# A mixture-of-experts layer that adds its gated expert rows up in DRAM by accumulating scatters

## What is computed

```python
top_logit, top_e = lax.top_k(logits, TOP_K)
gates = jax.nn.softmax(top_logit, axis=-1)
...
xs = xf[tok]
hu = lax.ragged_dot(xs, w_gate_up, group_sizes) + b_gate_up[e_sorted]
gate = jnp.minimum(hu[:, :D_FF], SWIGLU_LIMIT)
up = jnp.clip(hu[:, D_FF:], -SWIGLU_LIMIT, SWIGLU_LIMIT)
act = (up + 1.0) * gate * jax.nn.sigmoid(SWIGLU_ALPHA * gate)
y = lax.ragged_dot(act, w_down, group_sizes) + b_down[e_sorted]
y = y * g_sorted[:, None].astype(y.dtype)
out = jnp.zeros_like(xf).at[tok].add(y)
...
h = layer_norm(ALPHA_RES * h + ffn, ln2_g[l], ln2_b[l])
```

## Time and profile before

| what | value |
|---|---|
| median of 3 runs | 4528.06 us (4527.1 to 4535.33) |
| profiled execution: span | 4529.3 us |
| busy share of the span: PE, DVE, ACT, POOL | 95%, 68%, 40%, 22% |
| mean granted TensorE clock | 0.972 |
| projection; attention; routing; experts; last stage, ends in the profile | about 643; 1840; 1854; 4387; 4529 us |
| DMA over the span | 665.72 MB, 147 GB/s |

### The profile page before, as it was taken

How to read it: one execution, slowest core, us unless ns; L and a number is a source line. 1 busy time by engine, 2 the same in 40 slices (tenths; PEclk the granted TensorE clock), 3 DMA queues, 4 the chain that set the end, 5 groups by cost and what they waited for, 6 DMA issues and landing times. The chain is left out here.

```text
span 4529.3 us, 70549 instructions
## 1 busy us (share of the span) xinstructions
PE 4289.9 (95%) x24356; PEld 3153.5 (70%) x24356; DVE 3076.1 (68%) x4861; ACT 1817.6 (40%) x2677; POOL 1010.1 (22%) x1152
## 2 busy tenths in 40 slices
PE   8999988999999998699999999999999999999987
PEld 4444434444444454599989889899999999999961
DVE  2587867878888873555556556666676777777768
ACT  1222223443434433233434444444445555555530
POOL 1111101221111122211112212222222222222235
PEclk9999989999999999799999999999999999999986
DMA  6443330120110010544555456474657667667668
GB/s 194 126 122 92 87 101 16 30 27 21 18 23 16 14 27 19 148 158 148 174 168 190 155 183 220 162 250 161 237 197 239 208 230 241 219 234 237 212 214 362
DMA packets 534140, 665.72 MB, mean 147 GB/s; under 512 B 64416, under 2 KB 402592, under 8 KB 533952
## 3 DMA queue, kind: packets, MB, share of 16 engines
q1 hardware_dynamic: 419664, 501.02, 34.7%
q10 hardware_dynamic: 87744, 77.15, 5.4%
q0 software_dynamic: 26576, 85.56, 5.0%
HBM read 543.61 MB, written 120.03 MB: 147 GB/s over the span
## 5 line engine op out<-in xcount | busy, mean ns | idle before, releaser
L2000 PE MATMUL gu<-x_hi,w_hi 128*128 128x240 f32 (+8 forms) x4096 | 1196.5, 292 | 4.1 <-issue 4.1
L2003 PE MATMUL gu<-x_lo,w_hi 128*128 128x240 f32 (+8 forms) x4096 | 1195.5, 292 | 0.5 <-issue 0.5
L2004 PE MATMUL gu<-x_hi,w_lo 128*128 128x240 f32 (+8 forms) x4096 | 1194.1, 292 | 0.0
L2106 DVE TENSOR_TENSOR w_lo<-w_raw,w_hi 128x2048 fp32r<-128x2048 f32 x386 | 874.6, 2287 | 414.1 <-ACT w_hi L2190 386.2
L2190 ACT ACTIVATE w_hi<-w_raw 128x2048 fp32r<-128x2048 f32 x386 | 726.8, 1908 | 207.4 <-PE gu L2004 132.0
L2000 PEld LDWEIGHTS gu<-x_hi,w_hi 128*128 128x128 f32 x4096 | 774.7, 189 | 4.5 <-issue 4.3
L2003 PEld LDWEIGHTS gu<-x_lo,w_hi 128*128 128x128 f32 x4096 | 773.3, 189 | 1.1 <-issue 0.9
L2004 PEld LDWEIGHTS gu<-x_hi,w_lo 128*128 128x128 f32 x4096 | 773.8, 189 | 0.0
L1972 POOL TENSOR_TENSOR a_lo<-up,a_hi 128x384 fp32r<-128x384 f32 x256 | 396.6, 1549 | 1177.8 <-ACT a_hi L2202 1177.8
L570 PE MATMUL proj_acc<-w_in_sb,hT 128*128 128x512 f32 (+1 forms) x1280 | 499.0, 537 | 0.7 <-ACT hT L586 0.7
L2000 PE MATMUL yp<-w_hi,a_hi 128*128 128x512 f32 x1088 | 445.6, 410 | 2.3
(11 more groups left out here) (316 smaller groups left out, 5878.6 us busy)
## 6 DMA issues: line engine op xcount, KB each, us to landing
w_raw<-w_gate_up SPq DMA_DIRECT2D x258, 1024.0 KB, 7.6
w_raw<-w_down SPq DMA_DIRECT2D x128, 1024.0 KB, 8.1
y_dram<-y_rows ACTq DMA_DIRECT2D x128, 256.0 KB, 2.6
y_dram<-zeros ACTq DMA_DIRECT2D x12, 2688.0 KB, 15.5
h_blk<-h_dram SPq DMA_DIRECT2D x32, 512.0 KB, 8.7
qi_dram<-qi_stage ACTq DMA_DIRECT2D x16, 640.0 KB, 3.2
x_in<-x SPq DMA_DIRECT2D x16, 512.0 KB, 6.1
w_in_sb<-w_in SPq DMA_DIRECT2D x4, 2048.0 KB, 14.2
```

The costliest lines, as they stand in the source:

```text
L2000: op = nc.tensor.matmul(out, s_hi_, m_hi, start=(n == 0), stop=False)
L2003: nc.tensor.matmul(out, s_hi_, m_lo, start=False, stop=False)
L2004: op = nc.tensor.matmul(out, s_lo_, m_hi, start=False, stop=(n == len(pairs) - 1))
L2106: nc.vector.tensor_tensor(w_lo[:, c % 2, cols], raw[:, c % 3, cols], w_hi[:, c % 2, cols].bitcast(F32), ALU.subtract).then_inc(s_lo, 1)
```

## The change

Every token gets a row in a new DRAM tensor, `sums`, in which `h1` is written first, beside its place of old. A list entry now holds the token and its gate, divided by `ALPHA_RES`. ACT multiplies a strip by the gates when it copies it out of PSUM, and POOL, in place of ACT and SP, adds the strip to its tokens' rows of `sums` by indirect scatters that accumulate. The unused places of a list name rows behind the last token, with gate 0. `hold` fetches a visit's tokens and gates out of the list buffer before the next gather overwrites it, and waits until the last visit's scatters have landed; it and the gather now stand before j = 3 of POOL's loop. For the third tile of rows, SP loads the list in four pieces and a small table of constants (`load_third`). The last stage loads `sums` where it gathered, PE makes the bias alone, and the finish on DVE has two operations where it had three. The first norm's factor `ALPHA_RES` is divided out of the variance's epsilon. What served the old way (the positions, their round trip through DRAM, the zeros in `y_dram`) goes.

The diff, cut to its core:

```diff
 project_stage, on ACT
-                        nc.scalar.dma_start(D_["y"][row:row + SHARE, :].rearrange("(p n) (c d) -> p (n c) d", n=SHARE_N, d=P),
-                                            zeros[0:shape[0]].unsqueeze(1).broadcast_to(shape)).then_inc(s_clear, 16)
 attend_stage, on SP
-                sp.dma_start(D_["lists"][0:EXPERTS * SEQ, :].rearrange("(p n) o -> p (n o)", p=P),
-                             res[:, 0:EXPERTS * SEQ // P].bitcast(I32)).then_inc(s_clear, 16)
...
+                sp.dma_start(D_["lists"].rearrange("(p a n) o -> p a (n o)", p=CLEARED, a=2),
+                             res[0:CLEARED, 0:2 * ROWS].bitcast(I32).unsqueeze(1).broadcast_to(shape)
+                             ).then_inc(s_clear, 16)
+                for name in ("h1", "sums"):
+                    sp.dma_start(D_[name][SEQ:, :].rearrange("(m p) n -> p m n", p=P),
+                                 res[:].unsqueeze(1).broadcast_to([P, 1 + ROWS // P, D])).then_inc(s_clear, 16)
...
-                    sp.dma_start(D_["h1"][b * P:(b + 1) * P, :], h1[:]).then_inc(s_h1st, 16)
+                    for name in ("h1", "sums"):
+                        sp.dma_start(D_[name][b * P:(b + 1) * P, :], h1[:]).then_inc(s_h1st, 16)
 attend_stage, on DVE (weigh)
+                    nc.vector.tensor_copy(entry[:, :, 0], token[:, b:b + 1].broadcast_to([P, TOP_E]))
...
+                    nc.vector.tensor_scalar(entry[:, :, 1].bitcast(F32), e_gate, e_inv, 1.0 / ALPHA_RES,
+                                            ALU.mult, ALU.mult).then_inc(s_at, 1)
 experts_stage, on SP (store_third and the round trip of the positions go)
+                def load_third(v):
+                    at = look_up(sp, v, 1, MOST)
                     rest, few = (look_up(sp, v, what, 1) for what in (2, 3))
+                    if not first(v):
+                        sp.wait_ge(s_hold, v)
                     for i in range(4):
+                        row = at + 2 * P + i * FEW - rest * ((i - i % 2) * FEW) - few * (i % 2 * FEW)
+                        sp.dma_start(third[i * FEW:(i + 1) * FEW], D_["lists"][bass.ds(row, FEW), :]
+                                     ).then_inc(s_third, 16)
+                    sp.dma_start(spot[:], A["spots"][bass.ds(rest + few, 1)].rearrange("o p j n -> (o p) j n")
+                                 ).then_inc(s_third, 16)
 
                 def body(v):
...
                         if first(v) and c == 0:
                             sp.wait_ge(s_who, 16)
+                            load_third(0)
                         if first(v) and c == 1:
                             sp.wait_ge(s_x, 48)
-                        if not first(v) and c in (3, 4):
-                            store_third(v - 1, 2 if c == 3 else 5)
+                        if c == 5:
+                            load_third(v + 1)
                         chunk(v, c, e)
 experts_stage, on POOL
+                def hold(v):
+                    if not first(v):
+                        pool.wait_ge(s_yst[0], 32 * v)
+                        pool.wait_ge(s_yst[1], 32 * v)
+                        pool.wait_ge(s_yst[2], 48 * v)
+                    pool.wait_ge(s_third, 80 * v + 80)
+                    nc.gpsimd.tensor_tensor(scaled[:], spot[:, :, 0], third[:, 0:1].broadcast_to([P, 3]), ALU.mult)
+                    for h in range(2):
+                        nc.gpsimd.tensor_scalar(at_main[:, :, h], who[:, 0:2, 0], 2.0, float(h), ALU.mult, ALU.add)
+                    nc.gpsimd.tensor_copy(gate_now[:, 0:2], who[:, 0:2, 1].bitcast(F32))
+                    nc.gpsimd.tensor_copy(gate_now[:, 2:3], third[:, 1:2].bitcast(F32))
+                    pool.drain()
+                    nc.gpsimd.tensor_tensor(at_third[:], scaled[:], spot[:, :, 1], ALU.add).then_inc(s_hold, 1)
+                    pool.drain()
+                def scatter(v, n):
+                    pool.wait_ge(s_y, 6 * v + n + 3)
+                    nc.gpsimd.tensor_tensor(idle[:, n:n + 1], zero[:, 0:1], zero[:, 0:1], ALU.add)
+                    if n % 3 < 2:
+                        parts = [(halves, at_main[:, n % 3, n // 3:n // 3 + 1], y[:, n % 3])]
+                    elif n == 2:
+                        parts = [(quarters, at_third[:, w:w + 1], y[:, 2, w * BANK // 2:(w + 1) * BANK // 2])
+                                 for w in range(2)]
+                    else:
+                        parts = [(halves, at_third[:, 2:3], y[:, 2])]
+                    for rows, at, part in parts:
+                        nc.gpsimd.indirect_dma_start(rows, bass.IndirectOffsetOnAxis(ap=at, axis=0), part, None,
+                                                     compute_op=ALU.add).then_inc(s_yst[n % 3], 16)
                 def body(v):
-                    gather(v + 1)
+                    if not first(v):
+                        scatter(v - 1, 5)
                     for j in range(J):
+                        if j == 3:
+                            hold(v)
+                            gather(v + 1)
                         pool.wait_ge(s_ah, 8 * v + j + 1)
                         nc.gpsimd.tensor_tensor(a_lo[:, j], up[:, j % 2], a_hi[:, j].bitcast(F32), ALU.subtract)
                         nc.gpsimd.tensor_copy(a_rest[:, j], up[:, j % 2, 2 * P:2 * P + REST]).then_inc(s_al, 1)
+                    for n in range(5):
+                        scatter(v, n)
 experts_stage, on ACT (store)
-                        act.wait_ge(s_yst[slot], (32, 32, 192)[slot] * v + (0, 0, 0, 16, 16, 128)[n])
-                    nc.scalar.activation(y[:, slot], yp[:, n % 2], ACT.Copy).then_inc(s_y, 1)
-                    if n % 3 < 2:
-                        act.wait_ge(s_y, 6 * v + n + 3)
-                        nc.scalar.dma_start(
-                            D_["y"][bass.ds(v * ROWS + (n % 3) * P, P), (n // 3) * BANK:(n // 3 + 1) * BANK], y[:, slot]
-                        ).then_inc(s_yst[slot], 16)
+                        act.wait_ge(s_yst[slot], (32, 32, 48)[slot] * v + (0, 0, 0, 16, 16, 32)[n])
+                    if n == 0:
+                        act.wait_ge(s_hold, v + 1)
+                    nc.scalar.activation(y[:, slot], yp[:, n % 2], ACT.Copy, scale=gate_now[:, slot:slot + 1]
+                                         ).then_inc(s_y, 1)
 combine_stage, on SP (AHEAD is 6)
                     if t >= AHEAD:
-                        sp.wait_ge(s_tot, t - AHEAD + 1)
-                    sp.dma_start(h1[:, t % AHEAD], D_["h1"][t * P:(t + 1) * P, :]).then_inc(s_h1[t % AHEAD], 16)
+                        sp.wait_ge(s_st[slot], 16 * (t // AHEAD))
+                    sp.dma_start(total[:, slot], D_["sums"][t * P:(t + 1) * P, :]).then_inc(s_in[slot], 16)
 combine_stage, on POOL
-                    for k in range(TOP_E):
-                        nc.gpsimd.indirect_dma_start(
-                            rows[:, t % AHEAD, k], None, D_["y"],
...
 combine_stage, on DVE
-                    nc.vector.scalar_tensor_tensor(total[:, slot], h1[:, at], ALPHA_RES, acc[:, t % SUMS],
-                                                   ALU.mult, ALU.add).then_inc(s_tot, 1)
+                    nc.vector.tensor_tensor(row, row, acc[:, slot], ALU.add).then_inc(s_tot, 1)
...
+                    nc.vector.scalar_tensor_tensor(row, row, small[:, slot, 12:13], gain[:], ALU.subtract, ALU.mult)
+                    dve.drain()
                     dve.wait_ge(s_rstd, t + 1)
-                    nc.vector.tensor_scalar(total[:, slot], total[:, slot], small[:, slot, 12:13], small[:, slot, 15:16],
-                                            ALU.subtract, ALU.mult)
-                    dve.drain()
-                    nc.vector.tensor_tensor(total[:, slot], total[:, slot], gain[:], ALU.mult)
-                    dve.drain()
-                    nc.vector.tensor_tensor(total[:, slot], total[:, slot], bias[:], ALU.add).then_inc(s_out, 1)
+                    nc.vector.scalar_tensor_tensor(row, row, small[:, slot, 15:16], bias[:], ALU.mult, ALU.add
+                                                   ).then_inc(s_out, 1)
```

More of the change, by code:

```diff
@@ L90, in project_stage @@
     GAPS = 16
-    CLEARS = 12
-    SHARE = (MAX_VISITS - EXPERTS) * ROWS // CLEARS
-    SHARE_N = next(n for n in range(1, SHARE + 1) if SHARE % n == 0 and SHARE // n <= P)
-    assert SHARE * CLEARS == (MAX_VISITS - EXPERTS) * ROWS
     CHUNKS = [(n * BANK, min(BANK, IN_W - n * BANK)) for n in range(5)]
@@ L1609, in half @@
                             act.wait_ge(s_clear, CLEARS)
-                        wait(act, s_h1st, 16 * k)
+                        wait(act, s_h1st, 32 * k)
                         wait(act, s_ht, 2 * k)
@@ L1765, in _ @@
                 nc.vector.tensor_scalar(here[:], until[:], visit_no[:], None, ALU.is_gt)
-                nc.vector.scalar_tensor_tensor(table[:, 1], expert_no[:], float(SEQ), table[:, 1], ALU.mult, ALU.add)
+                nc.vector.scalar_tensor_tensor(table[:, 1], expert_no[:], float(LISTED), table[:, 1], ALU.mult, ALU.add)
```

(17 more changed lines are left out.)

219 lines of the change are left out of this document (63 added, 156 removed).

## The result

The changed kernel takes **4538.2 us** (median of 20 runs, 4530.8 to 4548.6) against 4528.6 us for the kernel before (20 runs beside them): a ratio of **1.0019**, 95% interval 1.0012 to 1.0026. The forecast was 4512 us, faster. It is slower by a fifth of a per cent. This small change of the time hides two large ones of opposite sign. The profiled execution spans 4536.6 us, 7.3 more than that of before.

What follows compares the result with a forecast made beforehand. PE was taken to bound the experts, with POOL's `a_rest` last in its chain, and DMA the last stage. -35.8 + 4.5 + 11 + 2 + 2 = -16.3 us from 4528.06 gave 4512 us, range 4492 to 4550.

Steps and rivals of the forecast that it cites:

- Last stage: Stage after the experts: gathers go, DVE sets the pace at 5.62 us a tile; 142.2 to 106.4 us, gain 35.8.
- Seam: Between experts and last stage: POOL's last accumulating scatter must land; 8.6 us against 4.1, +4.5 us.
- Visits: Experts stage: POOL's block before j = 3 makes 12 width-240 visits 0.9 us late each; +11 us, bounds 0 and 64.
- `hold`, six small operations and two drains, about 1.4 us: POOL before j = 3: estimated from `who_now`, 0.19 us apiece, plus gaps; part of a 12.1 us block against 10.38 of room.
- 0.81 us of DVE's slack: DVE's idle time before the gate of j = 7 in a width-240 visit, taken off the 1.7 us overrun, leaving 0.9.
- Start and attention: Before the first gate: +2 us at the experts' start (0 to 4) and +2 in attention (0 to 6).
- the first (the block fits): Rival, POOL before j = 3: chain 0.9 us shorter, no visit loses; 4501 us, 4495 with short landings; chance 0.17.
- The second (slow list load): Rival, POOL before j = 3: list load waits 5.17 us, narrow visits lose 3.9 to 5.4; 4548 to 4565 us; chance 0.17.
- Its break-even: The second rival's deciding point: from 2.3 us lost per narrow visit, or 13.5 us for POOL's whole block.
- The third (rows land late): Rival, scatters: landing takes 15 us, delaying the fourth strip's copy; 32 us more in visits, 7.5 at seam; 4552 us; chance 0.16.
- The fourth: Rival, last stage: it does not quicken, as loads wait for stores in SP's queue; +19.5, 4548 us; chance 0.05.
- the lower bound of the visits: Visits' loss of 0, if `hold` and the register load take 2.2 us together instead of 3.1.

Runs made afterwards that it cites:

- the four kernels with the tile `held`: Changed kernel, list copied to its own tile, gather at the visit's head: 4617.3 us; ahead of strip 4's scatter: 4499.3; plus semaphore: 4481.6; plus drainless `hold`: 4482.1.
- the run with more drains: The changed kernel with two more small operations, a drain behind each, at the end of `hold`: 4648.7 us, ratio 1.0255.

## Why the prediction was wrong

**Last stage**: right, by its steps. Forecast 106.4 us with a tile of 5.62 and 13.4 us up to the first sum; measured 106.6, 5.57 and 13.5. No wait of DVE for a load; restoring the third operation cost what the tile grew by.

**Seam**: right in its sum, 9.1 us against a forecast of 8.6, but by luck, for its terms are off both ways. From the last copy out (4420.96) to the issue of the last scatter it was 1.8 us, as the scatter of strip 4 stands ahead of it on POOL; the landing took 5.4 us, not 7.5; from there to the next stage it was 1.9. The forecast had 0.7 and 0.4 for the first and the last of these. The rule on adding transfers (the Trainium skill, Collectives: The Full Stack, "The bandwidth ceiling: the fold count and why AG ≠ RS ≠ AR") would have an add move at half a copy's rate. The trace agrees with it for this last scatter, 5.4 against 2.7 us, and not for those in the visits, where the add lands 1.2 to 1.3 times as late.

**Visits**: here the forecast failed, in one term. The mechanism was the one named: `hold` and the gather before j = 3, queued behind them `a_lo` of j = 3, behind that DVE's `up` of j = 5, in the width-240 visits above all (those of width 256 lost 0.4 us). The step that was mis-sized is "`hold`, six small operations and two drains, about 1.4 us". It took **3.44** us. The other parts came out as put down or below: register load and gap 1.60 (forecast 1.7; the second drain fills it), list load to the last gather issue 7.40 (7.76), `a_lo` and `a_rest` 1.21 (1.25). With the small gaps that is 13.67 against 12.1. Half of the 2.0 us that `hold` was longer stands there without any weight rest: with `hold` before j = 2 it took 2.45 us, as its first drain alone leaves POOL idle for 0.99 us, where the forecast had 1.4 for the six operations and both drains together. The other half is the weight rest. The forecast took `hold`'s operations from rows in which no weight rest ran beside them, though the text behind that sum weighed the rule of the shared port (the Trainium skill, SBUF — State Buffer, "Who interferes with whom") for `a_lo` and for the scatters' operations. The trace agrees with that rule where it was not applied: `at_third` ends with the weight rest, at 1.22 us instead of 0.20, and without drains at 2.13. Since the drain and the weight rest pass at the same time, taking out the drains alone left `hold` at 3.47 us.

The second half of the miss is what lateness costs. The forecast let 0.81 us of DVE's slack stand against 1.7 us of overrun, 0.9 us a visit. The overrun was 13.67 - 10.38 = 3.3 us, so 2.5 was to be expected, and 3.0 was lost: some 0.3 us came on top behind the gate of j = 7 (from there to the end of `a_rest` it takes 5.51 us instead of 5.20); the last 0.2 is not accounted for. In visits 20 and 31 PE's stop also brought its clock to half for some 3 us; those two lost 4.6 and 4.8 us. In sum: ten visits at 3.0, two at some 4.7, three of width 256 at 0.4 make some 40 us; the others changed by less than 1 us, either way. One premise, that a visit can only lose as PE is full, did not hold either: in the four kernels with the tile `held` the products follow each other faster and full visits are shorter than before.

**Start and attention**: forecast +4, measured -2. It can't be told apart from chance: in the changed kernel and the seven variants that leave the head of the visit alone, with the same code up to there, the first gate lay between 1886.5 and 1894.4 us.

**The rivals**: the first (the block fits) is not what happened, but what happens when `hold` is moved one j: 4501 us, the number it gave, in part by luck: the visits there still take 5.3 us more than before, and the start took 3 us less where the rival had 4 more. The second (slow list load) did not happen: the wait was 1.54 us. The forecast's reason for the short wait, that the list load goes out ahead of chunk 5, is borne out by the run with more drains, where it goes out behind that chunk and waits 5.07 us. Its break-even, a block of 13.5 us, decided all the same: the block was 13.67. The third (rows land late) did not: copies waited for a scatter eight times, 2.3 us at most, and the visits don't care. The fourth did not: DVE never waited for a load. So the chance of a slower kernel was there for other reasons than the true one; a shorter `hold` made the lower bound of the visits, but no longer one was in the upper.

## What to carry to other kernels

A block put into a full chain has a place as well as a length: read the room at that place in the narrowest case, and price each of its operations in the company it will have there, since small ones can grow six- to ten-fold beside a two-input operation of DVE. Cutting a block in two and moving one half by one step was worth more here than shortening it. When work is moved back to a place that used to be free, look at what has been queued there since.

## What the runs showed of the hardware

- A drain on POOL right behind an indirect scatter held POOL until the scatter had landed: 8.61 us to the next issue with the drain, always 1.77 to 1.79 us behind the landing, and 1.52 us with a semaphore of the operation that had to be done.
- DVE and POOL shut each other out both ways, and the one shut out waits for a run of the other's operations, not for one alone: a weight rest of 2.28 us took 4.77 beside two `a_lo`, a multiplication of 0.56 us took 2.22, and a POOL copy of 0.24 us took 2.29.
- The list load, 3 KB, waited for 1.54 us when issued 1.6 us ahead of a 2 MB weight load, and for 5.07 us when issued 1.3 us behind it.
- After a stop of PE of 2.0 to 2.5 us the granted clock sometimes fell to half for some 3 us, which cost the visit 1.5 to 1.6 us: in 2 of 12 width-240 visits of the changed kernel, in 5 of 12 without `hold`'s drains, in 6 of 12 with three `up` buffers and with the list load before j = 2. What decides it the runs don't show.
- An accumulating scatter landed 1.2 to 1.3 times as late as the same scatter without the add while weights were loaded (8.3 against 6.5 us for strip 0), and twice as late with no weight load beside it (5.4 against 2.7 us).
- The same matrix products of 240 columns, at the full granted clock, followed each other in 111.7 ns in four kernels and in 113.3 in ten; the four share a 24-byte tile declared ahead of the products' operands and the gather at the head of the visit. The cause is open.
